# An opening of one core: the scale row's lower half by column quarters, and the first two half units of the MLP interleaved

## The chip, the cores and the metric

The kernel runs on one core of one Trainium2 chip. A core has a matrix engine (TensorE, PE in the rows; PEld is its weight load), VectorE (DVE), ScalarE (ACT), GpSimd (POOL), and SyncE (SP), whose in-order queue issues the loads from memory. Engines run beside each other and meet at semaphores. The metric is the device time of one execution in microseconds (us), here the median of three.

## The reference

Two layers, 256 tokens, 2048 channels, all in fp32. Each layer has a mixer and an MLP, and each of these begins with a norm that a conditioning vector modulates:

```python
cond = jax.nn.silu(c)
for i in range(DEPTH):
    mod = jnp.einsum('bd,sdk->bsk', cond, ada_w[i]) + ada_b[i]       # 2048 x 12288 weights for each layer
    shift_t, scale_t, gate_t = jnp.split(mod[:, 0], 3, axis=-1)
    shift_m, scale_m, gate_m = jnp.split(mod[:, 1], 3, axis=-1)
    h = modulate(rmsnorm(x, norm_g[i, 0]), shift_t, scale_t)          # h * (1 + scale) + shift
    y = pool_mixer(h, ...) if i == 0 else retention(h, ...)
    x = x + gate_t[:, None, :] * y
    h = modulate(rmsnorm(x, norm_g[i, 1]), shift_m, scale_m)
    x = x + gate_m[:, None, :] * sq_relu_mlp(h, mlp_w1[i], mlp_w2[i])
return rmsnorm(x, final_g)
```

The change touches the modulation of the first layer's MLP: `shift_m` and `scale_m` for channels 0 to 1023, and the first columns of `h @ mlp_w1[0]`.

## The kernel before, in words

**Products.** A product of fp32 by fp32 is made of three matmuls on rounded halves (`h_lo` by `w_hi`, `h_hi` by `w_lo`, `h_hi` by `w_hi`, L701). Weights come in chunks of 512 KB: two K tiles of 128 rows by 512 columns, in a ring of four buffers `raw`. ScalarE rounds a chunk into `w_hi` (`hi`, L1167), VectorE subtracts it into `w_lo` (`lo`, L1598), and TensorE runs 12 matmuls on it (2 K tiles, 2 token tiles, 3 products). SP loads the chunk four places on once `lo` of a chunk is done (`load_chunk`, L515).

**The conditioning rows.** A row of 1024 outputs of `cond @ ada_w` is summed from 16 pieces of 512 KB (128 K rows by 1024 columns). They pass through 12 slots: 4 in `ada_raw`, 8 in memory that `h_hi` and `h_lo` (`ada_early_h`) or `a_hi` and `a_lo` (`ada_early_a`) use later. SP loads a piece once the piece 12 places before it is consumed (`load_early`, L521). Some K tiles are multiplied on TensorE (`shared_rows`, L883: two matmuls of 32x512 for a piece, `cond` as the stationary operand), the others are added up on VectorE (`early`, L1628, one instruction of 128x1024), and TensorE sums VectorE's part over the partitions once (`row_blocks`, L853). `LOW_SCALE_PE` (L151) lists the K tiles of the scale row that go to TensorE. Segment 3 is 32 such pieces: 0 to 15 the shift row, 16 to 31 the scale row, both for channels 0 to 1023. In this text scale piece 0 is piece 16 of the segment. When a row is full, ScalarE copies it out (`copy_rows`, L1274), TensorE transposes it (`column`, L953), and VectorE adds the bias (`take_half`, L1737) and makes the gain (`gains`, L1933).

**The norm.** `norm_fill(f)` (L974) transposes and scales two K tiles of x on TensorE (four matmuls of 128x128), with two banks `tb` in turn; ScalarE copies each out (`transposed_x`, L1212) and later modulates it in place (`norm_bank`, L1227), and VectorE splits it into `h_hi` and `h_lo` (`split_h`, L1971). The first K tiles have a shorter way (`split_first`, L1943).

**The order.** After the pooling mixer, TensorE runs the shift pieces, fills 0 to 6 with the scale pieces among them, the column, fill 7, and then 8 parts of the first MLP group. A part is a half unit: 512 columns over the lower 8 K tiles, so 4 chunks (`half_unit`, L750). During the parts 32 more pieces (segment 4) come in among the chunks; most are added up on VectorE. Then come the whole units of both layers. The order on every engine is written out by hand.

## Time and profile before

| | |
|---|---|
| Three runs | 2336.54, 2337.79 (median), 2337.93 us |
| Span of the profiled execution | 2336.1 us; the runs are 0.5 to 1.9 us above it |
| TensorE busy over the span | 2251.9 us (96%) |
| VectorE, ScalarE busy | 1681.1 us (72%), 1084.2 us (46%) |
| Moved by DMA | 664.21 MB, mean 284 GB/s |
| Start of the first MLP part | 188.1 us into the span |

The profile holds one execution. Its rows are read for two things: where TensorE, whose rows make up most of the chain that ends last, stands still, and what it does there besides products. In this kernel both lie in the stretch before 188 us; behind it TensorE is busy nearly without a gap. The DMA queues move 400 GB/s and more up to about 262 us, and less behind that.

### The profile page before, as it was taken

What the parts mean: (1) busy time and instruction counts of PE and PEld (TensorE: products, weight loads), DVE (VectorE), ACT (ScalarE), POOL (GpSimd) and SP (SyncE); (2) the same over time, 40 slices, a digit from 0 to 9 for tenths busy, and PEclk for the clock granted to TensorE, in tenths of its full rate; (3) what the DMA queues carried; (4) which work ended last, traced back from release to release, by engine and by line L of the source; (5) the groups of instructions that cost most, each with busy time, mean ns of one, the idle gap of its engine ahead of it and who ended that gap; (6) DMA issues with size and microseconds to landing.
All of it is one profiled execution on the core that took longest, in us unless ns stands there. A gap on an engine that the chain in (4) does not pass through costs nothing.

```text
span 2336.1 us, 28515 instructions
## 1 busy us (share of the span) xinstructions
PE 2251.9 (96%) x10033; PEld 1817.7 (78%) x10033; DVE 1681.1 (72%) x1814; ACT 1084.2 (46%) x1342; POOL 139.9 (6%) x249
## 2 busy tenths in 40 slices
PE   4489999999999999999999999999999999999998
PEld 2147788888888887888888888887888888888887
DVE  4668889788887898777676767677877555555557
ACT  2324554544544545444454444555553453453454
POOL 0000000100100100001000001000100000000000
PEclk9689999999999999999999999999999999999999
DMA  9999989998998977888766887876997776776774
GB/s 400 415 413 393 339 297 328 364 367 277 368 334 292 362 281 231 303 264 275 246 233 215 299 260 244 273 239 202 333 359 248 235 230 195 226 232 191 232 228 152
DMA packets 276674, 664.21 MB, mean 284 GB/s; under 512 B 21768, under 2 KB 22200, under 8 KB 269632
## 3 DMA queue, kind: packets, MB, share of 16 engines
q1 hardware_dynamic: 260320, 611.92, 75.8%
q0 software_dynamic: 15328, 49.87, 6.2%
q8 instruction: 75, 1.23, 0.2%
q10 hardware_dynamic: 896, 0.75, 0.1%
q14 instruction: 55, 0.45, 0.1%
HBM read 638.30 MB, written 24.14 MB: 284 GB/s over the span
## 4 chain that ended last, share of the span: by engine, by line
PE 88%; DMA 2%; DVE 2%; ACT 1%; issue 0%; POOLq 0%; POOL 0%; SPq 0%; DVEq 0%; ACTq 0%
PE acc L701 86%; DMA raw<-in_mlp_w 2%; PE acc L1122 1%; DVE w_lo L1601 1%; PE score_ps L1109 0%; ACT w_hi L1173 0%; DVE ada_acc L1607 0%; PE score_ps L908 0%; PE tb L848 0%; DVE ev L1903 0%; PE tb L983 0%; DVE x L1907 0%; DVE scratch L1773 0%; DVE scratch L1768 0%; PE mod_ps L856 0%
## 5 line engine op out<-in xcount | busy, mean ns | idle before, releaser
L1601 DVE TENSOR_TENSOR w_lo<-raw,w_hi 128x1024 fp32r<-128x1024 f32 x775 | 943.3, 1223 | 558.6 <-ACT w_hi L1173 555.5
L1173 ACT ACTIVATE w_hi<-raw 128x1024 fp32r<-128x1024 f32 x775 | 821.8, 1061 | 1094.8 <-PE acc L701 971.5
L701 PE MATMUL acc<-w_hi,h_lo 128*128 128x512 f32 x1788 | 698.5, 391 | 2.6 <-issue 1.6
L701 PE MATMUL acc<-w_hi,h_hi 128*128 128x512 f32 x1788 | 695.8, 389 | 0.0
L701 PE MATMUL acc<-w_lo,h_hi 128*128 128x512 f32 x1788 | 695.8, 389 | 0.0
L701 PE MATMUL acc<-w_hi,a_lo 128*128 128x512 f32 x1308 | 511.6, 391 | 0.4 <-DVE w_lo L1601 0.4
L701 PE MATMUL acc<-w_lo,a_hi 128*128 128x512 f32 x1308 | 510.3, 390 | 0.0
L701 PE MATMUL acc<-w_hi,a_hi 128*128 128x512 f32 x1308 | 510.0, 390 | 0.0
L701 PEld LDWEIGHTS acc<-w_hi,h_lo 128*128 128x128 f32 x1788 | 335.7, 188 | 75.1 <-issue 4.1
L701 PEld LDWEIGHTS acc<-w_hi,h_hi 128*128 128x128 f32 x1788 | 335.7, 188 | 70.0
L701 PEld LDWEIGHTS acc<-w_lo,h_hi 128*128 128x128 f32 x1788 | 335.8, 188 | 68.5
L1607 DVE SCALAR_TENSOR_TENSOR ada_acc<-ada_raw,cond,ada_acc 128x1024 f32<-128x1024 f32 x239 | 305.1, 1279 | 10.9 <-DMA ada_raw<-in_ada_w 10.5
L701 PEld LDWEIGHTS acc<-w_hi,a_lo 128*128 128x128 f32 x1308 | 246.6, 189 | 57.7 <-issue 6.1
L701 PEld LDWEIGHTS acc<-w_hi,a_hi 128*128 128x128 f32 x1308 | 246.4, 188 | 51.5
L701 PEld LDWEIGHTS acc<-w_lo,a_hi 128*128 128x128 f32 x1308 | 246.6, 189 | 50.9
L2436 POOL DMA_DIRECT2D square_blocks<-ev x112 | 61.3, 553 | 717.4 <-DVE ev L2161 701.8
L1607 DVE SCALAR_TENSOR_TENSOR ada_acc<-ada_early_h,cond,ada_acc 128x1024 f32<-128x1024 f32 x36 | 44.9, 1281 | 24.4 <-DMA ada_early_h<-in_ada_w 24.3
L878 PE MATMUL mod_ps<-ada_early_h,cond 128*32 128x512 f32 x88 | 18.7, 935 | 28.5 <-DMA ada_early_h<-in_ada_w 28.5
L1470 ACT ACTIVATE ev<-ev 128x512 f32<-128x512 f32 x64 | 36.7, 626 | 0.0
L2167 DVE TENSOR_TENSOR a_lo<-ev,a_hi 128x512 fp32r<-128x512 f32 x56 | 35.8, 680 | 0.0
L1204 ACT ACTIVATE sq_junk<-x 128x512 bf16<-128x512 f32 x45 | 27.8, 618 | 15.6 <-DMA x<-in_x 7.5
L2161 DVE STREAM_TRANSPOSE ev<-ev 128x1024 f32<-128x1024 f32 x28 | 34.7, 1238 | 0.0
(216 smaller groups left out, 912.9 us busy)
## 6 DMA issues: line engine op xcount, KB each, us to landing
raw<-in_mlp_w SPq DMA_DIRECT2D x512, 512.0 KB, 5.1
ada_raw<-in_ada_w SPq DMA_DIRECT2D x248, 512.0 KB, 6.6
raw<-in_ret_w_in SPq DMA_DIRECT2D x192, 512.0 KB, 4.6
ada_early_h<-in_ada_w SPq DMA_DIRECT2D x32, 1024.0 KB, 13.4
raw<-in_ret_w_out SPq DMA_DIRECT2D x64, 512.0 KB, 4.4
ada_raw<-in_ada_w SPq DMA_DIRECT2D x16, 1024.0 KB, 12.5
square_blocks<-ev POOLq DMA_DIRECT2D x112, 128.0 KB, 4.8
ev<-square_blocks POOLq DMA_DIRECT2D x28, 512.0 KB, 6.4
```

Of the source, the lines that this page charges most:

```text
L701: mm = nc.tensor.matmul(acc[pair][t][:], l[:, CK * c + j, tok], w[:, slot, j, :], start=first and j == 0 and i == 0, stop=last and j == CK ...
L878: mm = nc.tensor.matmul(bank[32 * b:32 * b + 32, :], cond[:, k:k + 1].to_broadcast([P, 32]), raw_rows[:, b * NB:(b + 1) * NB], start=first ...
L1122: mm = nc.tensor.matmul(acc[pair][t][:], probs_r[:, half, columns:columns + P], v[:, v_t, :], start=first and i == 0, stop=last and i == 2)
L1173: nc.scalar.activation(w_hi[:, o % RING], raw[:, o % RING], ACT.Copy).then_inc(hi_ready, 1)
L1204: nc.scalar.activation(sq_junk[:, t, :], x[:, t, block_ * NB:(block_ + 1) * NB], ACT.Square, scale=D ** -0.5, accum_out=ssq[:, t, block_:b ...
L1470: nc.scalar.activation(squares_of(u, t, turns), squares_of(u, t, turns), ACT.Square).then_inc(sq_done, 1)
L1601: nc.vector.tensor_tensor(w_lo[:, o % RING], raw[:, o % RING], w_hi[:, o % RING].bitcast(F32), ALU.subtract).then_inc(lo_ready, 1)
L1607: nc.vector.scalar_tensor_tensor(out=part, in0=raw_rows, scalar=cond[:, k:k + 1], in1=part, op0=ALU.mult, op1=ALU.add).then_inc(ada_done, 1)
L2161: nc.vector.transpose(blocks_of(w), blocks_of(w)).then_inc(sq_turned, 1)
L2167: nc.vector.tensor_tensor(by_blocks(a_lo, w, t), turned(w, t), by_blocks(a_hi, w, t).bitcast(F32), ALU.subtract).then_inc(tlo, 1)
L2436: pool.dma_start(there[:, :, q, :].rearrange("r j n -> j r n"), blocks_of(w)[32 * q:32 * q + 32].rearrange("p (r n) -> p r n", r=4)).then_ ...
```

## The change

The 16 pieces of the scale row are cut another way. A piece is now two K tiles by 512 columns, so that 8 pieces fill channels 0 to 511 (the first quarter) and 8 more fill channels 512 to 1023 (the second). Ten of the 16 go to TensorE (before, six), six to VectorE (before, ten). TensorE writes the even and the odd K tiles to separate blocks of a bank, 32 partitions each, and VectorE adds the two blocks with the bias in `take_quarter`, once for each quarter. VectorE's own pieces take two instructions of 128x512, the second of which waits for the first. The first quarter opens K tiles 0 to 3 of h; the four chunks that need only these (the first two of part 0 and of part 1) are loaded among the scale pieces and run first, on both accumulators. The second quarter's pieces, fills 4 to 7 and a second column stand between and behind the chunks.

```diff
-LOW_SCALE_PE = (1, 3, 7, 11, 14, 15)
+LOW_SCALE_PE = (1, 3, 5, 6, 7, 9, 11, 13, 14, 15)
+KQ = KT // 2
+SCALE_SUM_AT = (5, 13)
+FIRST_PAIR = ((0, 0), (0, 1), (1, 0), (1, 1), (0, 2), (0, 3), (1, 2), (1, 3))
+PAIR_LOADED_BEHIND = {22: 0, 23: 1, 26: 2, 28: 3}
+LOW_TURN = 3 * SEG + KT + KQ
...
-            return slot, (ada_early_h if g < 4 * SEG else ada_early_a)[:, slot - RING]
+            return slot, (ada_early_h if g < LOW_TURN else ada_early_a)[:, slot - RING]
...
+                if seg == 3 and a >= KT:
+                    q, i = (a - KT) // KQ, (a - KT) % KQ
+                    sp.dma_start(to.rearrange("p (k n) -> p k n", k=2),
+                                 ada_flat[1, 2 * i * P:(2 * i + 2) * P, 1, q * NB:(q + 1) * NB].rearrange(
+                                     "(k p) n -> p k n", p=P)).then_inc(ada_in[slot], 16)
+                    return
...
             for a in range(SEG):
                 load_early(3, a)
-                if a == 30:
-                    load_chunk(0, first_part(0))
+                if a in PAIR_LOADED_BEHIND:
+                    load_chunk(PAIR_LOADED_BEHIND[a], pair_chunk(PAIR_LOADED_BEHIND[a]))
...
+            def second_quarter():
+
+                scale_rows(30, SEG)
+                norm_fill(4)
+                column(score_ps)
+                norm_fill(5)
...
+            def scale_rows(a0, a1):
+                for a in range(a0, a1):
+                    g, j = 3 * SEG + a, a - KT
+                    q, i = j // KQ, j % KQ
+                    bank, b = ((score_ps, 2), (mod_ps, 0))[q]
+                    if j == SCALE_SUM_AT[q]:
+                        n.add(AD=DVE_BEFORE[g] - n.n["AD"])
+                        pe.wait_ge(ada_done, n.n["AD"])
+                        nc.tensor.matmul(bank[32 * b:32 * b + 32, :], ones[:, 0:32],
+                                         ada_acc[:, AW + q * NB:AW + (q + 1) * NB], start=False, stop=False).then_inc(row_mm, 1)
+                        n.add(RM=1)
+                    if ON_PE[g]:
+                        first = PE_BEFORE[g] == PE_BEFORE[g - i]
+                        if first and q:
+                            pe.wait_ge(row_ready, 3)
+                        slot, raw_rows = early_slot(3, a)
+                        pe.wait_ge(ada_in[slot], early_loads(3, a))
+                        for h in range(2):
+                            mm = nc.tensor.matmul(bank[32 * (b + h):32 * (b + h) + 32, :],
+                                                  cond[:, 2 * i + h:2 * i + h + 1].to_broadcast([P, 32]),
+                                                  raw_rows[:, h * NB:(h + 1) * NB], start=first, stop=i == KQ - 1)
...
+            scale_rows(16, 20)
             pe.wait_ge(gate_ready, 4)
             pe.wait_ge(diag_ready, 1)
-            for f in range(KT // 2 - 1):
-                norm_fill(f)
-                if f in (1, 3):
-                    shared_rows(3, 15 + f, 17 + f)
-                elif f == 5:
-                    shared_rows(3, 20, 28)
-            shared_rows(3, 28, SEG)
+            norm_fill(0)
+            scale_rows(20, 22)
+            norm_fill(1)
+            scale_rows(22, 24)
             column(score_ps)
-            norm_fill(KT // 2 - 1)
-
+            norm_fill(2)
+            norm_fill(3)
+            scale_rows(24, 26)
             n.add(HT=CH)
+            pe.wait_ge(evac, 4 * TT)
+            between = {1: lambda: scale_rows(26, 28), 2: lambda: scale_rows(28, 30), 3: second_quarter,
+                       5: lambda: norm_fill(6), 7: lambda: norm_fill(7)}
+            for s, (i, c) in enumerate(FIRST_PAIR):
+                pe.wait_ge(lo_ready, n.of("U") * HALF + (s + 1))
+                if s == 0:
+                    first_chunk()
+                else:
+                    ready_h(c)
+                    chunk(c, h_hi, h_lo, i, c == 0, c == HALF - 1, slot=s % RING)
+                if s in between:
+                    between[s]()
...
+            def scale_piece(a):
+                q, i = (a - KT) // KQ, (a - KT) % KQ
+                part = ada_acc[:, AW + q * NB:AW + (q + 1) * NB]
...
+                even, odd = raw_rows[:, 0:NB], raw_rows[:, NB:2 * NB]
+                if i:
+                    nc.vector.scalar_tensor_tensor(out=part, in0=even, scalar=cond[:, 2 * i:2 * i + 1], in1=part,
+                                                   op0=ALU.mult, op1=ALU.add).then_inc(scale_step, 1)
...
+                dve.wait_ge(scale_step, scale_steps[0])
+                nc.vector.scalar_tensor_tensor(out=part, in0=odd, scalar=cond[:, 2 * i + 1:2 * i + 2], in1=part,
+                                               op0=ALU.mult, op1=ALU.add).then_inc(ada_done, 1)
```

On TensorE, between the shift pieces and the first matmul of the MLP, this stands in the kernel before (`tb<-diag,x` x4 is one fill, `score_ps<-ada_...,cond` x2 one scale piece, `ada_acc,ones` the sum of VectorE's part, `ident,seg_row` the column):

```order
L983 MATMUL tb<-diag,x 128x128 x8
L908 MATMUL score_ps<-ada_early_h,cond 32x512 x2
L983 MATMUL tb<-diag,x 128x128 x8
L908 MATMUL score_ps<-ada_early_h,cond 32x512 x2
L983 MATMUL tb<-diag,x 128x128 x8
L908 MATMUL score_ps<-ada_early_h,cond 32x512 x2
L908 MATMUL score_ps<-ada_raw,cond 32x512 x2
L983 MATMUL tb<-diag,x 128x128 x4
L856 MATMUL score_ps<-ada_acc,ones 32x512 x2
L908 MATMUL score_ps<-ada_early_h,cond 32x512 x4
L959 MATMUL score_ps<-ident,seg_row 128x128 x4
L983 MATMUL tb<-diag,x 128x128 x4
```

and this in the changed kernel:

```order
L959 MATMUL score_ps<-ada_early_h,cond 32x512 x4
L1033 MATMUL tb<-diag,x 128x128 x4
L949 MATMUL score_ps<-ada_acc,ones 32x512
L959 MATMUL score_ps<-ada_early_h,cond 32x512 x2
L1033 MATMUL tb<-diag,x 128x128 x4
L959 MATMUL score_ps<-ada_early_h,cond 32x512 x4
L1009 MATMUL score_ps<-ident,seg_row 128x128 x4
L1033 MATMUL tb<-diag,x 128x128 x8
L959 MATMUL mod_ps<-ada_raw,cond 32x512 x2
```

Eight fills, six pieces, the sum and the column stood ahead of the MLP; now it is four fills, six pieces (five of the first quarter, one of the second), half the sum and a column. The rest stands among the products. Behind the fourth chunk TensorE of the changed kernel has the second quarter's end (the last rows of the fourth chunk, then two pieces, fill 4, the second column, fill 5, and the fifth chunk):

```order
L721 MATMUL acc<-w_lo,h_hi 128x512
L721 MATMUL acc<-w_hi,h_hi 128x512
L959 MATMUL mod_ps<-ada_early_a,cond 32x512 x4
L1033 MATMUL tb<-diag,x 128x128 x4
L1009 MATMUL score_ps<-ident,seg_row 128x128 x4
L1033 MATMUL tb<-diag,x 128x128 x4
L721 MATMUL acc<-w_hi,h_lo 128x512
```

In the kernel before there is nothing between the chunks there. On VectorE of the changed kernel the same place reads as follows (`w_lo` of two chunks, `take_quarter` and the gain, then the split of K tiles 4 and 5, `w_lo` of the sixth chunk, the split of K tiles 6 and 7, and three pieces of segment 4):

```order
L1684 TENSOR_TENSOR w_lo<-raw,w_hi 128x1024 x2
L1858 TENSOR_TENSOR mod_col<-score_ps,bias_col 128x4
L1860 TENSOR_TENSOR mod_col<-score_ps,mod_col 128x4
L2062 SCALAR_TENSOR_TENSOR gain_col<-mod_col,norm_col 128x4
L2102 CAST h_hi<-scratch 128x512
L2104 TENSOR_TENSOR h_lo<-scratch,h_hi 128x512
L1684 TENSOR_TENSOR w_lo<-raw,w_hi 128x1024
L2102 CAST h_hi<-scratch 128x512
L2104 TENSOR_TENSOR h_lo<-scratch,h_hi 128x512
L1693 TENSOR_SCALAR ada_acc<-ada_early_a,cond 128x1024
L1690 SCALAR_TENSOR_TENSOR ada_acc<-ada_early_a,cond,ada_acc 128x1024 x2
L1684 TENSOR_TENSOR w_lo<-raw,w_hi 128x1024
```

Before, the splits stood ahead of the pieces of segment 4, and `w_lo` of a chunk alternated with one piece of segment 4.

## Rows read from the trace of the kernel before

**Rows 1.** The page: shares of the chain that ended last, by engine.
```profile
PE 88%; DMA 2%; DVE 2%; ACT 1%; issue 0%; POOLq 0%; POOL 0%; SPq 0%; DVEq 0%; ACTq 0%
```
**Rows 2.** Timeline of PE: start, length, operation, count, [idle before, releaser].
```profile
167.17 1.92 PE L856 MATMUL score_ps<-ada_acc,ones 128*32 128x512 f32 x4 [4.37 <-DVE ada_acc L1607]
168.88 1.92 PE L908 MATMUL score_ps<-ada_raw,cond 128*32 128x512 f32 x4
170.73 2.86 PE L983 MATMUL tb<-diag,x 128*128 128x128 f32 x16
...
174.50 2.05 PE L983 MATMUL tb<-diag,x 128*128 128x128 f32 x16
176.48 1.05 PE L908 MATMUL score_ps<-ada_early_h,cond 128*32 128x512 f32 x4
...
182.37 1.05 PE L856 MATMUL score_ps<-ada_acc,ones 128*32 128x512 f32 x4
183.25 1.94 PE L908 MATMUL score_ps<-ada_early_h,cond 128*32 128x512 f32 x8
185.94 0.66 PE L959 MATMUL score_ps<-ident,seg_row 128*128 128x128 f32 x4 [0.75 <-ACT seg_row L1286]
186.44 1.06 PE L983 MATMUL tb<-diag,x 128*128 128x128 f32 x8
188.11 0.47 PE L742 MATMUL acc<-w_hi,h_hi 128*128 128x512 f32 x1 [0.62 <-DVE h_hi L1951]
...
190.93 0.39 PE L701 MATMUL acc<-w_hi,h_lo 128*128 128x512 f32 x1
```
**Rows 3.** Stretches: length, busy us (count) by engine, PE clock, DMA share, GB/s.
```profile
162.00:170.70 8.70, 4.33 (x12) 0.55 (x8) 7.83 (x15) 2.98 (x10) 1.15 (x1) 0.71 1.03 408
170.70:188.10 17.40, 16.05 (x98) 9.92 (x97) 13.92 (x16) 6.54 (x11) 0.00 (x0) 0.95 1.02 381
188.10:210.00 21.90, 21.89 (x97) 18.06 (x97) 20.89 (x24) 12.37 (x17) 0.00 (x0) 1.00 1.04 399
```
**Rows 4.** The chain in order of time, from 243.7 us: start, length, what.
```profile
243.72 9.45 DMA raw<-in_mlp_w
253.19 1.07 ACT w_hi L1173
254.28 1.24 DVE w_lo L1601
...
335.48 508.70 PE acc L701 x2244
```
**Rows 5.** Timeline of PE: the wait at the 25th chunk.
```profile
255.56 0.50 PE L701 MATMUL acc<-w_hi,h_lo 128*128 128x512 f32 x1 [0.54 <-DVE w_lo L1601]
```
**Rows 6.** Timeline of ACT: a chunk rounded, the row copied, two K tiles of x modulated.
```profile
182.97 1.05 ACT L1173 ACTIVATE w_hi<-raw 128x1024 fp32r<-128x1024 f32 x1
185.29 0.60 ACT L1286 ACTIVATE seg_row<-score_ps 128x512 f32<-128x512 f32 x1 [1.27 <-issue]
190.71 1.08 ACT L1235 ACTIVATE scratch<-scratch,mod_col,gain_col 128x256 f32<-128x256 f32 x2
```
**Rows 7.** Timeline of DVE: weights, column, gain, first modulation, splits.
```profile
184.06 1.23 DVE L1601 TENSOR_TENSOR w_lo<-raw,w_hi 128x1024 fp32r<-128x1024 f32 x1 [2.67 <-ACT w_hi L1173]
186.82 0.17 DVE L1744 TENSOR_TENSOR mod_col<-score_ps,bias_col 128x16 f32<-128x16 f32 x1
187.67 0.29 DVE L1951 CAST h_hi<-scratch 128x256 fp32r<-128x256 f32 x1
189.00 0.42 DVE L1977 CAST h_hi<-scratch 128x512 fp32r<-128x512 f32 x1
189.46 0.69 DVE L1979 TENSOR_TENSOR h_lo<-scratch,h_hi 128x512 fp32r<-128x512 f32 x1
207.36 2.60 DVE L1607 SCALAR_TENSOR_TENSOR ada_acc<-ada_raw,cond,ada_acc 128x1024 f32<-128x1024 f32 x2
```
**Rows 8.** Timeline of PE: two shorter waits.
```profile
130.99 1.06 PE L878 MATMUL mod_ps<-ada_raw,cond 128*32 128x512 f32 x8 [1.27 <-DMA ada_raw<-in_ada_w]
141.02 1.30 PE L856 MATMUL mod_ps<-ada_acc,ones 128*32 128x512 f32 x8 [2.31 <-DVE ada_acc L1607]
```
**Rows 9.** Stretches around these two waits, columns as in Rows 3.
```profile
124.70:141.70 17.00, 13.43 (x74) 8.18 (x76) 12.30 (x11) 3.09 (x4) 0.00 (x0) 1.00 1.01 417
141.70:145.10 3.40, 3.40 (x15) 1.17 (x8) 0.93 (x2) 0.00 (x0) 0.00 (x0) 0.50 1.02 408
```

More of the change, by code:

```diff
@@ L1635, in early @@
                         continue
+                    if seg == WIDE_SEGS and half:
+                        scale_piece(a)
+                        continue
                     if k:
@@ L2117, in _ @@
             diagonals()
-            early(3, 18, SEG)
-            n.add(U=2, TB=CH, GN=2)
+            early(3, 18, 24)
+            n.add(U=2, TB=2, GN=2)
             lo(0)
@@ L2122, in _ @@
             second_lo(0)
-            take_half(0)
-            gains(slice(0, KT // 2))
+            take_quarter(0)
+            gains(slice(0, KT // 4))
             split_first()
@@ L2127, in _ @@
             second_lo(1)
+            early(3, 24, 26)
+            lo(2)
+            early(3, 26, SEG)
+            lo(3)
+            lo(4)
+            take_quarter(1)
+            gains(slice(KT // 4, KT // 2))
+            n.add(TB=CH - 2)
             split_h(2)
-            lo(2)
+            lo(5)
             split_h(3)
-            lo(3)
             for i in range(PARTS):
```

108 lines of the change are left out of this document (80 added, 28 removed).

## The prediction, made before the changed kernel was run

> **What bounds the kernel now.** I read the chain by engine first [rows 1]: 88% of it is TensorE, 2% DMA. So a change counts by what it does to TensorE's last matmul. Then TensorE's timeline around the change [rows 2]. The reader is to see that from 170.73 to 188.11 us it has only two waits, 0.75 us for the copied row and 0.62 us for the first split of h; the rest of those 17.4 us is fills, scale pieces, the sum and the column, end to end. The stretch view says the same: 16.05 us busy of 17.40, and 4.33 of 8.70 in the stretch before it [rows 3]. The long wait of this opening, 4.37 us, ends at 167.17, where the shift row waits for VectorE [rows 2], and the change leaves everything up to there as it is.
>
> Behind 188.11 the products run without a gap (21.89 of 21.90 us [rows 3]) at 0.2267 us a matmul (508.70 us by 2244 [rows 4]), 2.72 us a chunk. There the DMA queues are full too, 399 GB/s at a busy share of 1.04 [rows 3], and chunks and the pieces of segment 4 come hardly faster than TensorE uses them: at the 25th chunk it waits 0.54 us for `w_lo` [rows 5], and the chain runs through that chunk's load, 9.45 us from issue to landing, its rounding and its subtraction [rows 4]. So the opening has two limits close together. TensorE has work for nearly all of it, and a TensorE that came to the parts earlier would meet the same bytes at the same rate, and wait at the 25th chunk.
>
> The Trainium skill speaks against the first half of this. Its page "Perfetto Trace Analysis", section "Identifying the Most-Contended Engine", says that a busy share of the matmul row is no measure of how near TensorE is to its limit, since matmuls are pipelined, and that the weight loads are. By it, TensorE with its loads at 9.92 of 17.40 us [rows 3] would have room here. What decides for me is not the share but the starts: each group in the timeline begins where the one before it stops issuing (174.50, then 176.48 [rows 2]), with no releaser named.
>
> **The change, part by part.**
>
> *Durations, by starts.* A piece takes 0.94 us (two from 183.25 to 185.19), a fill 1.0 (two from 174.50 to 176.48), a sum of two matmuls 0.88 (182.37 to 183.25), a column 0.50 (185.94 to 186.44), the first chunk 2.82 (188.11 to 190.93) [rows 2]. At half clock (0.50 from 165.7 on; it is 0.95 in the mean of 170.7 to 188.1 [rows 3]) a piece took 1.85 (168.88 to 170.73) [rows 2].
>
> *Work added on TensorE.* Ten pieces instead of six: 4 x 0.94 = 3.8 us. A second column: 0.5. The sums are two matmuls in both. The first work behind 170.73 is now a piece, which half clock stretches by 0.9 us, where the first two fills lost 0.8 (2.79 against 2.0): 0.1. Together 4.4 us, and none of it is beside other work, since TensorE is in order and has no wait left that it could fill but the 1.4 us above.
>
> *Where the first chunk comes.* From 170.73: pieces 1 and 3 to 173.5, fill 0 to 174.5, half the sum and piece 5 to 175.9, fill 1 to 176.95, pieces 6 and 7 to 178.8. ScalarE copies the row (0.60 [rows 6]) to 179.5, the column is done at 180.0; TensorE goes on with fills 2 and 3 and piece 9 to 183.0. Meanwhile ScalarE has rounded chunk 1 behind fill 1's copy (0.97, to 178.5 [rows 6]), and VectorE subtracts it (1.15, to 179.7), makes `w_hi` of the second chunk and half its `w_lo` (to 181.0), three additions and the gain in place of 0.4 us (0.7, to 181.7), the modulation and the first cast (to 182.5 [rows 7]). So the first chunk starts at 183.0, 5.1 us earlier than 188.11.
>
> *And the fifth.* 2.82 for the first, 2.72 for each of three, piece 11 (0.94) behind the second, half a sum and piece 13 (1.4) behind the third: the fourth ends at 196.35. Pieces 14 and 15 to 198.25. Now the second quarter: copy to 198.9, fill 4 to 199.25, column to 199.75, fill 5 to 200.8; on VectorE take and gain to 200.4, on ScalarE the modulation of two K tiles (1.0 [rows 6]) to 201.4, on VectorE cast and subtraction (0.42 and 0.69 [rows 7]) to 202.6. TensorE waits 1.8 us. The fifth chunk starts at 202.6; before, it started at 190.93 + 3 x 2.72 = 199.1. The head start of 5.1 us has become 3.5 us behind.
>
> *The next three.* VectorE does `w_lo` of the sixth chunk only behind that first split, then the second split, to 205.7; TensorE is there at 205.3 and waits 0.4. Behind this stand three pieces of segment 4 (0.7, then 1.3 each, half of 2.60 [rows 7]) ahead of `w_lo` of the seventh chunk, done at 210.0; TensorE, with fill 6 behind the sixth, is there at 209.4 and waits 0.6. With fill 7 behind the eighth chunk the ninth starts at 216.6. Before, it started at 190.93 + 7 x 2.72 = 210.0. That is 6.6 us later, which the other count confirms: 4.4 of work, plus waits of 0.7 + 1.8 + 0.4 + 0.6 = 3.5 in place of 1.4, is 6.5.
>
> *What is given back.* A TensorE that is 6.6 us late doesn't wait at the 25th chunk: 0.5 less. Net 6.1 us.
>
> *Loads.* The scale pieces' runs in memory are 2 KB as a chunk's are, where they were 4 KB. The stretch of pieces alone moved 408 GB/s, the mixed one 399 [rows 3]; if all of that is the chunks' doing, a 2 KB load costs 0.06 us more, 1.0 us for 16, and nothing if it isn't. Against it, 170.7 to 188.1 moved only 381 GB/s [rows 3], since slots came free late; the new order issues the four chunks among the pieces, where their ring is free, and could win back (408 - 381) x 17.4 / 408 = 1.2 us. Both ends together move the landings by -1.2 to +1.0 us, and with TensorE behind its data that costs nothing. I take 0.
>
> *VectorE's split pieces* are a kind the trace doesn't show (128x512, twice). Bounds: 0.64 each, half of 1.28, up to 1.3 each, if a short one costs as much as a long. Three of them lie ahead of each sum; by the upper end the first sum is late by up to 1 us. I take 0.69, as the 128x512 subtraction [rows 7].
>
> *A wait that the change adds:* `take_quarter` in VectorE's order, with the column behind it on TensorE. Queued behind it: `w_lo` of chunks 6 and on, segment 4's pieces, and through these SP's later loads. The chain above counts it. Loads slip by up to 4 us, which TensorE's own 6.6 covers.
>
> **Sum.** 2336.1 (the span) + 6.1 = 2342.2, and the median run is 1.7 above the span: 2343.9.
>
> **The rivals.**
>
> *The clock falls at the new wait.* A wait of 1.27 us left the clock at 1.0, one of 2.31 was followed by 3.4 us at 0.50, that is 1.2 instead of 2.4 GHz [rows 8, 9]. The new 1.8 us lies between. If it falls, 3.4 us pass at half rate: 1.7 more, 2345.6; for a stretch twice as long 3.4, 2347.3. Against it: TensorE was dense before this wait. The Trainium skill, "TensorE: Matmul & The Clock Gate", section "HAM oscillation — how this bites in real kernels", says that a wait between bursts of matmuls is paid twice, the second time by a throttled clock. By that rule this rival is the likelier; the trace has it both ways.
>
> *The new waits don't arise.* If splits, copies and columns fit beside the fills better than by my count, 4.4 - 1.4 + 0.7 - 0.5 is left: 3.2 us, 2341.0. This is the least that the added matmuls leave. It would show as a fifth chunk at about 200.8.
>
> *The head start is kept (faster).* TensorE reaches the first chunk 5.1 us earlier, and if pieces, fills and column slip in beside the products and the loads are 1.2 us earlier and no longer limit, the end comes up to 5.1 earlier: 2332.7. It decides from the point where the fifth chunk starts ahead of 199.1. Against it: 12 matmuls more than before have to run (8 for pieces, 4 transposes) on an engine whose rows follow end to end [rows 2], and even if they cost nothing, the 25th chunk's load gives no more than 1.2 + 0.5 us, 2336.1. The Trainium skill's rule on the busy share, above, would be the reason for this rival; the starts of the rows are the reason that I hold it unlikely.
>
> **How the numbers follow.** My forecast 0.50, the clock 0.17, no new waits 0.20, head start kept 0.08 (half of it capped by the loads, hence no change), something that I don't see 0.05. A change of 0.2%, 4.7 us, is about what a measurement of this kernel tells from none. Slower by more than that: forecast and clock, less the lower edge of the forecast: 0.62. Within: no waits, that edge, the capped case: 0.29. Faster: 0.09. The range goes from 2338.0 (the case without waits, less 3.0 us: the added 4.4 us of work mis-sized, or the loads' 1.2 and 0.5 won) to 2347.8 (the clock down for the longer stretch, and 0.5 for the runs' spread).
>
> **What the new profile would show.** Right: first matmul of the MLP at 182 to 184 us; two more waits of TensorE behind it, the largest of 1 to 2.5 us ahead of the fifth chunk; the ninth chunk at 215 to 218; no wait at the 25th; ten pieces of 0.94 us. Wrong: a fifth chunk before 199, pieces that take less among the products, or a gap of TensorE behind 220 us. A clock of 0.50 behind 200 us means the first rival.

## The result and the profile after

| | before | after |
|---|---|---|
| Median (lowest to highest) of 10 runs each | 2337.75 us (2336.54 to 2338.72) | 2342.68 us (2341.65 to 2345.39) |
| Ratio, with its 95% interval | | 1.0022 (1.0013 to 1.0031) |
| Profiled execution: span, mean clock | 2336.1 us, 0.987 | 2343.1 us, 0.985 |
| First, fifth, ninth chunk of the MLP starts | 188.1, 199.1, 210.0 us | 181.5, 202.5, 216.8 us |

The kernel became slower by 4.9 us; the forecast was 6.1. The profiled execution of the changed kernel is one of its slower ones (2344.9 us with what lies around its span): its span is 7.0 us above that of the kernel before. At 900 us it is 5.9 us behind (the same transposes start at 900.06 there and at 894.12 before), and the rest comes with a second stretch at half clock behind that, where the kernel before stayed at 1.00 (columns as in [rows 3]):

```profile
902.80:906.20 3.40, 3.40 (x9) 2.63 (x8) 3.33 (x10) 1.53 (x5) 0.55 (x1) 0.50 0.97 336
```

The chain by engine has lost its DMA share, 2% in [rows 1]:

```profile
PE 91%; DVE 1%; issue 1%; ACT 0%; POOLq 0%; POOL 0%; DVEq 0%; ACTq 0%
```

The timeline of PE, which answers to [rows 2] and [rows 5]. Columns are start, length, operation, count, [idle before, releaser]; L959 is a scale piece, L1033 a fill, L949 the sum, L1009 the column:

```profile
167.08 1.07 PE L880 MATMUL score_ps<-ada_acc,ones 128*32 128x512 f32 x2 [4.37 <-DVE ada_acc L1690]
167.11 1.07 PE L959 MATMUL score_ps<-ada_early_h,cond 128*32 128x512 f32 x2
...
170.66 1.95 PE L1033 MATMUL tb<-diag,x 128*128 128x128 f32 x8
172.54 0.62 PE L949 MATMUL score_ps<-ada_acc,ones 128*32 128x512 f32 x1
...
175.47 1.91 PE L959 MATMUL score_ps<-ada_early_h,cond 128*32 128x512 f32 x8
178.12 0.66 PE L1009 MATMUL score_ps<-ident,seg_row 128*128 128x128 f32 x4 [0.75 <-ACT seg_row L1349]
...
181.48 0.50 PE L762 MATMUL acc<-w_hi,h_hi 128*128 128x512 f32 x1
...
195.91 1.91 PE L959 MATMUL mod_ps<-ada_early_a,cond 128*32 128x512 f32 x8
197.75 1.16 PE L1033 MATMUL tb<-diag,x 128*128 128x128 f32 x8
198.75 0.60 PE L1009 MATMUL score_ps<-ident,seg_row 128*128 128x128 f32 x4
199.18 1.06 PE L1033 MATMUL tb<-diag,x 128*128 128x128 f32 x8
202.45 0.47 PE L721 MATMUL acc<-w_hi,h_lo 128*128 128x512 f32 x1 [2.21 <-DVE h_lo L2104]
...
216.76 0.48 PE L721 MATMUL acc<-w_hi,h_lo 128*128 128x512 f32 x1
```

The reader is to see three things. The first scale pieces start at 167.11, 0.03 us behind the shift row's sum, in the midst of it. The first chunk comes 6.6 us sooner than before, with no wait ahead of it. Then one wait of 2.21 us stands between fill 5 and the fifth chunk. The stretches, to set against [rows 3] and [rows 9] (length, busy us and count by engine, PE clock, DMA share, GB/s):

```profile
181.50:202.45 20.95, 18.74 (x88) 11.97 (x87) 11.39 (x19) 8.05 (x13) 0.00 (x0) 1.00 1.04 398
203.07:206.48 3.41, 3.41 (x10) 2.64 (x9) 3.32 (x5) 2.36 (x3) 0.00 (x0) 0.50 1.04 377
216.76:256.00 39.24, 39.24 (x175) 31.57 (x174) 37.74 (x33) 18.18 (x22) 0.00 (x0) 1.00 1.03 394
```

Right behind the wait TensorE ran at 0.50 for 3.41 us, which costs 1.7. From the ninth chunk to 256 us it is busy for 39.24 of 39.24 us; the kernel before was busy for 38.70 us of the same stretch. So the wait at the 25th chunk [rows 5] is gone.

### The profile page after: what moved, and what is told of

It reads as the page before. It is cut to its first block, busy times and chain, and to the rows that moved or that the text cites. A ratio compares the mean times of both kernels' runs of the same rounds, so it can differ in the third digit from the quotient of the medians.

```text
span 2343.1 us, 28564 instructions
## 1 busy us (share of the span) xinstructions
PE 2258.1 (96%) x10053; PEld 1820.5 (78%) x10053; DVE 1676.9 (72%) x1821; ACT 1083.8 (46%) x1343; POOL 139.2 (6%) x249
## 4 chain that ended last, share of the span: by engine, by line
PE 91%; DVE 1%; issue 1%; ACT 0%; POOLq 0%; POOL 0%; DVEq 0%; ACTq 0%
PE acc L721 88%; PE acc L1185 1%; PE score_ps L1172 0%; PE tb L1033 0%; DVE ada_acc L1690 0%; PE tb L872 0%; DVE ev L2028 0%; PE mod_ps L959 0%; DVE w_lo L1684 0%; PE score_ps L932 0%; PE mod_ps L880 0%; ACT w_hi L1236 0%; DVE x L2032 0%; PE score_ps L959 0%; PE tb L857 0%
## 5 line engine op out<-in xcount | busy, mean ns | idle before, releaser
L1690 DVE SCALAR_TENSOR_TENSOR ada_acc<-ada_early_h,cond,ada_acc 128x1024 f32<-128x1024 f32 x30 | 37.2, 1280 | 24.0 <-DMA ada_early_h<-in_ada_w 24.0
```

What stands on the lines that cost most here:

```text
L1690: nc.vector.scalar_tensor_tensor(out=part, in0=raw_rows, scalar=cond[:, k:k + 1], in1=part, op0=ALU.mult, op1=ALU.add).then_inc(ada_done, 1)
```

## The experiments

Each was timed in five rounds beside the kernel before; "above" is its median less that of the kernel before in the same job. An interval of a ratio is 0.0009 wide to each side, 2.1 us, so a difference of under 2 us between two variants is not told by their medians, and what is said of it below comes from the traces. The ninth chunk's start is that of the profiled execution; the chunks behind it run without gaps in all of them, but where it is said. In some profiled executions the shift row's sum stands at 165.3 to 165.5 us instead of 166.8 to 167.3, since the clock did not fall at 141 us there [rows 9]; these have a star, and up to 1.7 us of their earlier ninth chunk is this.

| kernel | median, us | above | ratio (95%) | ninth chunk | longest wait behind the first chunk, and the clock behind it |
|---|---|---|---|---|---|
| the changed kernel | 2342.68 | 4.93 | 1.0022 (1.0013 to 1.0031) | 216.8 | 2.21, 0.50 |
| q2_early | 2339.54 | 1.69 | 1.0008 (0.9999 to 1.0017) | 213.2 | none, 1.00 |
| fill6_in_wait* | 2344.25 | 6.40 | 1.0025 (1.0016 to 1.0035) | 214.6 | 1.35, 1.00 |
| fill6_pieces_later* | 2343.41 | 5.81 | 1.0023 (1.0014 to 1.0032) | 213.0 | 1.32, 1.00 |
| seven_on_pe | 2342.00 | 4.15 | 1.0018 (1.0009 to 1.0027) | 214.9 | 2.22, 0.50 |
| seven_filled* | 2342.10 | 4.68 | 1.0022 (1.0013 to 1.0031) | 214.3 | 0.63, 1.00 |
| q2_and_seven* | 2339.91 | 2.06 | 1.0008 (0.9999 to 1.0017) | 211.9 | 0.61, 1.00 |
| pair_before | 2337.26 | -0.16 | 1.0001 (0.9992 to 1.0010) | 209.5 | none, 1.00 |
| no_pair | 2341.54 | 4.12 | 1.0016 (1.0007 to 1.0025) | 214.9 | 1.32, 1.00 |
| no_pair_four* | 2340.57 | 3.15 | 1.0014 (1.0005 to 1.0023) | 212.1 | 1.72, 1.00 |
| q2_four | 2340.81 | 3.21 | 1.0012 (1.0003 to 1.0022) | 212.0 | 1.41, 1.00 |
| q2_eight_four | 2338.94 | 1.34 | 1.0008 (0.9999 to 1.0017) | 213.1 | 2.18, 0.50 |
| q2_balanced | 2338.86 | 0.98 | 1.0006 (0.9997 to 1.0015) | 211.9 | 0.91, 1.00 |

### q2_early: the second quarter one chunk sooner

```diff
             def second_quarter():
-                scale_rows(30, SEG)
+                scale_rows(28, SEG)
                 norm_fill(4)
                 column(score_ps)
-                norm_fill(5)
-            between = {..., 2: lambda: scale_rows(28, 30), 3: second_quarter, ...}
+            between = {..., 2: second_quarter, 3: lambda: norm_fill(5), ...}
# ScalarE: copy_rows and transposed_x(4) ahead of hi(4); VectorE: take_quarter and gains ahead of lo(4)
```

> The changed kernel, with the second quarter finished one chunk sooner: its last two K tile pieces, fill 4 and the column stand behind the third chunk (they stood behind the fourth), fill 5 alone behind the fourth; ScalarE copies that row ahead of rounding the next chunk, and VectorE takes the quarter ahead of the subtraction of the fifth chunk. TensorE's work is the same. My theory (the 4.9 us are TensorE's work plus the one wait of 2.21 us ahead of the fifth chunk, and the clock that falls behind it): the wait is under 0.5 us, the clock stays at 1.00 until 210 us, the ninth chunk starts at about 212.8 instead of 216.8, and the end comes 2.2 us earlier, 3.9 in executions that had the lowered clock: 2339 to 2340.5, that is 1.5 to 2.8 us above the kernel before. Rival one (the pieces' 2 KB runs and the moved loads set the time): the wait goes, but a new one for w_lo of the fifth to ninth chunk takes its place, and the end is as in the changed kernel, 2342 to 2343. Rival two (the order of fills and columns doesn't matter since later buffers absorb it): also 2342 to 2343, with the ninth chunk earlier and a wait behind it.

Measured: 1.69 us above the kernel before, where the changed kernel is 4.93. No run of the one lies among those of the other (at most 2340.73, at least 2341.65). The waits of TensorE from 160 to 860 us (us in total, times, longest):

```profile
PE score_ps L879 <- DVE ada_acc L1689: 4.4, 1, 4.4
PE score_ps L1008 <- ACT seg_row L1348: 0.7, 1, 0.7
```

Nothing else is left, and the stretch around the later chunks stands at full clock:

```profile
198.00:213.50 15.50, 15.50 (x80) 13.02 (x79) 15.33 (x16) 9.94 (x14) 0.00 (x0) 1.00 1.03 386
```

The ninth chunk starts at 213.2, 3.6 us sooner. So about 3.2 of the 4.9 us, by the medians, were the wait ahead of the fifth chunk and what it drew after it. Both rivals are out.

### fill6_in_wait and fill6_pieces_later: filling the wait

```diff
# fill6_in_wait, on the changed kernel
                 norm_fill(5)
+                norm_fill(6)
-                       5: lambda: norm_fill(6), 7: lambda: norm_fill(7)}
+                       7: lambda: norm_fill(7)}
# fill6_pieces_later, on top of it; VectorE, for j in RING..30
-                    early(4, late_summed(j - 1), late_summed(j))
+                    early(4, max(1, late_summed(j - 1) - 2), max(1, late_summed(j) - 2))
```

> The changed kernel, with fill 6 moved from behind the sixth chunk into the wait ahead of the fifth; nothing else. My theory: the fill (1.0 us) lies in the wait of 2.21 us, which becomes 1.2, and a wait of that length left the clock alone in the kernel before (1.27 us at 131 us). The gain is 1.0 us, and 1.7 more in executions in which the clock fell: 2340.0 to 2341.7. If it's the wait itself that draws the clock down whatever its length, 0.50 shows behind it here too and the gain is 1.0 us alone. If waits of TensorE in this place don't set the end (the rival: loads do), the time is that of the changed kernel, 2342.7, and a wait shows up at the 25th chunk.

> fill6_in_wait, and VectorE keeps two pieces of segment 4 behind its old schedule until the last part, so one of them instead of three stands ahead of w_lo of the seventh chunk. My theory (the new wait of 1.35 us at the seventh chunk in fill6_in_wait is VectorE's queue, 3.3 us of pieces between a split and w_lo): w_lo of the seventh chunk is done 2.4 us earlier, that wait goes, the ninth chunk starts 1.3 us earlier and no other wait stands behind it: 1.3 us less than fill6_in_wait's profiled 2342.4, and 2341.0 to 2343.0 in the median, with fewer executions above 2344. If the seventh chunk's load is what w_lo waits for, the wait stays and the time is 2344.2. If slots that come free two pieces later hold the loads back, a wait shows at the 13th to 25th chunk.

Both missed. The first came out 1.6 us slower in the medians, where I had expected 1.0 less. Its runs scatter from 2341.46 to 2345.65, so the sign isn't certain. The profiled run is one of the faster ones (2342.40), so its trace doesn't tell what the slower ones lose; it shows why there was no gain:

```profile
200.80 0.47 PE L721 MATMUL acc<-w_hi,h_lo 128*128 128x512 f32 x1 [1.33 <-DVE h_lo L2105]
...
208.22 0.50 PE L721 MATMUL acc<-w_hi,h_lo 128*128 128x512 f32 x1 [1.35 <-DVE w_lo L1685]
```

The time that the fill had vacated behind the sixth chunk became a wait for `w_lo` of the seventh. The timeline of DVE names the queue in front of it, 3.3 us of segment 4:

```profile
203.64 0.75 DVE L1694 TENSOR_SCALAR ada_acc<-ada_early_a,cond 128x1024 f32<-128x1024 f32 x1
204.42 2.61 DVE L1691 SCALAR_TENSOR_TENSOR ada_acc<-ada_early_a,cond,ada_acc 128x1024 f32<-128x1024 f32 x2
206.95 1.22 DVE L1685 TENSOR_TENSOR w_lo<-raw,w_hi 128x1024 fp32r<-128x1024 f32 x1
```

With two of those pieces held back the wait is gone, and the ninth chunk starts at 213.0 instead of 214.6, as expected. But the shift row of segment 4 comes later by them, and TensorE pays there, mostly at 272.81:

```profile
272.81 1.05 PE L881 MATMUL mod_ps<-ada_acc,ones 128*32 128x512 f32 x4 [0.89 <-DVE ada_acc L1691]
```

Two waits of 0.28 and 0.89 us take back 1.2 of the 1.6 us, and the median, 2343.41, lies above the 2341.0 to 2343.0 that I had expected. Two pieces moved on VectorE cost TensorE nearly as much later as they gave.

### seven_on_pe, seven_filled, q2_and_seven: less work on TensorE

```diff
# seven_on_pe, on the changed kernel; q2_and_seven is the same on q2_early
-LOW_SCALE_PE = (1, 3, 5, 6, 7, 9, 11, 13, 14, 15)
-SCALE_SUM_AT = (5, 13)
+LOW_SCALE_PE = (1, 3, 7, 9, 11, 13, 15)
+SCALE_SUM_AT = (7, 15)
# fills 0 to 3 ahead of scale_rows(20, 24)
# seven_filled, on seven_on_pe, behind norm_fill(5)
+                for r in range(8):
+                    nc.tensor.matmul(mod_ps[:, ...], x[:, 0, ...], diag[:, 0, :], start=True, stop=True)
```

> The changed kernel with seven of the sixteen scale pieces on TensorE instead of ten (1, 3, 7, 9, 11, 13, 15; 5, 6 and 14 go back to VectorE, two instructions each), the sums at pieces 7 and 15, and fills 0 to 3 ahead of the first quarter's last pieces. My theory (TensorE's added work is on the path, 0.94 us a piece): three pieces less are 2.8 us less; VectorE has 4.7 us more, of which it had idle 4.95 and 6.19 us: a wait for its sum of up to 1 us at each of the two sums. The end is 1 to 2.8 us ahead of the changed kernel's: 2340 to 2341.7. The rival that TensorE's rows aren't full there (pieces run beside others, as pieces 1 and 3 did at 167 us beside the shift row): 0 to 0.5 us earlier, or later by the waits for VectorE, 2342 to 2344.

> Both edits together: the second quarter one chunk sooner, and seven pieces on TensorE. My theory adds the two: 2.2 + 1 to 2.8 us less than the changed kernel, with no lowered clock behind 200 us: 2337.5 to 2339.5, the level of the kernel before; it can't go below it by more than about 0.5 us, since the load of the 25th chunk then ends last again, with a wait of TensorE there of up to 1 us. If it does go below by 2 us or more, that limit by the loads is wrong.

> The kernel with seven scale pieces on TensorE (seven_on_pe), and behind fill 5 eight extra matmuls of 128x128 into a bank that nobody reads, 2 us of work in the wait of 2.22 us ahead of the fifth chunk. They add nothing to the path. It tells why seven_on_pe gained 0.7 us in the medians where its trace, set against the changed kernel's, shows TensorE 1.7 us earlier. My theory (the wait lets the clock fall, 1.6 us lost in 3.4 us at half rate, in all of its executions but in only some of the changed kernel's): the clock stays at 1.00 behind 200 us, and the median is 1.6 us less than seven_on_pe's 2342.0: 2340.4, with runs below its lowest, 2341.34. Rival (the clock isn't what hides the gain; data arrive too late for more): 2342, and a wait stands somewhere behind.

Three pieces less on TensorE, 2.8 us by my price, gave 0.7 us in the medians, and 2342.0 lies outside the expected 2340 to 2341.7. The waits of TensorE in seven_on_pe from 160 to 860 us:

```profile
PE acc L721 <- DVE h_lo L2103: 2.2, 1, 2.2
PE score_ps L949 <- DVE ada_acc L1750: 0.9, 1, 0.9
PE score_ps L1009 <- ACT seg_row L1348: 0.8, 1, 0.8
PE acc L762 <- DVE h_hi L2075: 0.6, 1, 0.6
```

New are the 0.9 for VectorE's sum and the 0.6 ahead of the first chunk; the wait ahead of the fifth chunk is as long as it was. The ninth chunk starts 1.8 us earlier than in the changed kernel. My guess that the lowered clock hid the rest fell with seven_filled: its clock stays at 1.00 behind 200 us, and the median is no lower. Its fifth chunk starts at 200.56, seven_on_pe's at 200.64, although its shift row stands 1.4 us earlier, and a wait of 0.46 follows at the seventh:

```profile
207.97 0.50 PE L721 MATMUL acc<-w_hi,h_lo 128*128 128x512 f32 x1 [0.46 <-DVE w_lo L1686]
```

So this variant is held by VectorE and the loads. Of the 1.7 us that a stretch at half clock costs, only 0.50 show between the fifth and the ninth chunk (13.80 us against 14.30 in seven_on_pe), mostly since a TensorE at full rate arrives at that `w_lo` too soon.

q2_and_seven expected the level of the kernel before and got no further than q2_early. Here the waits that took over are 1.22 us for the load of scale piece 9 and 1.06 for VectorE's sum; behind them the clock stood at 0.50 from 178.66 to 182.07:

```profile
173.65 0.62 PE L948 MATMUL score_ps<-ada_acc,ones 128*32 128x512 f32 x1 [1.06 <-DVE ada_acc L1749]
...
178.18 1.49 PE L958 MATMUL mod_ps<-ada_raw,cond 128*32 128x512 f32 x4 [1.22 <-DMA ada_raw<-in_ada_w]
```

### pair_before: the free pieces in the kernel before

```diff
-            shared_rows(3, 4, 16)
+            shared_rows(3, 4, 20)
...
             for f in range(KT // 2 - 1):
                 norm_fill(f)
-                if f in (1, 3):
-                    shared_rows(3, 15 + f, 17 + f)
-                elif f == 5:
+                if f == 5:
```

> The kernel before, with one edit: the scale pieces 1 and 3 run right behind the shift row's last piece, ahead of fill 0, as in the changed kernel. In the changed kernel those two ran beside the shift row's sum and last piece (all between 167.1 and 170.7 us) and cost nothing, since they write other blocks of 32 partitions. My theory: they are free here too, 1.9 us less on TensorE, so the first chunk starts at about 186.3 instead of 188.1; but the load of the 25th chunk then ends last, its wait grows from 0.54 to about 2.4 us, and the time is 2337.3, at most 0.5 less than before (or 1 more, if the clock falls behind that wait). Rival (TensorE's work alone sets the end, and loads follow the earlier start): 2335.9, and the wait at the 25th chunk stays at 0.5. Rival two (the pieces aren't free behind 128x512 work of their own row): first chunk at 188.1, 2337.8.

The pieces are free here too. The timeline of PE (L856 the shift row's sum, L908 pieces of both rows, L983 fills):

```profile
166.86 1.07 PE L856 MATMUL score_ps<-ada_acc,ones 128*32 128x512 f32 x2 [4.37 <-DVE ada_acc L1605]
166.89 1.07 PE L908 MATMUL score_ps<-ada_early_h,cond 128*32 128x512 f32 x2
...
170.45 6.53 PE L983 MATMUL tb<-diag,x 128*128 128x128 f32 x48
...
181.17 1.05 PE L856 MATMUL score_ps<-ada_acc,ones 128*32 128x512 f32 x4 [1.26 <-DVE ada_acc L1605]
...
183.66 1.05 PE L908 MATMUL score_ps<-ada_early_h,cond 128*32 128x512 f32 x4 [0.58 <-DMA ada_early_h<-in_ada_w]
```

What the fills gained, they wait for: 1.26 and 0.58 us, 1.84 in all, for 1.9 us of saved pieces. The first chunk starts at 187.6, and no difference from the kernel before can be told. The median hits the 2337.3 that I had expected, but by luck. I had the price right and its taker wrong: not the 25th chunk's load, but the sum and a scale piece, 6.5 us ahead of the first chunk. At the 25th chunk no wait of TensorE is listed, where I had expected 2.4 us: the rounding of that chunk, which waits for its load in both kernels, starts at 251.91 instead of 253.19. So the load followed the earlier start, as the rival had it. In the kernel before TensorE, VectorE and the loads all arrived at the scale row nearly together, though TensorE's rows showed no wait for the other two.

### no_pair and no_pair_four: without the interleaving

```diff
# no_pair, on the changed kernel
-FIRST_PAIR = ((0, 0), (0, 1), (1, 0), (1, 1), (0, 2), (0, 3), (1, 2), (1, 3))
+FIRST_PAIR = tuple((i, c) for i in range(2) for c in range(4))
-                scale_rows(30, SEG)
+                scale_rows(26, SEG)      # then fill 4, column, fills 5 and 6
+            between = {1: second_quarter, 2: lambda: norm_fill(7)}
# no_pair_four, on top of it, in scale_rows
+                        nth = PE_BEFORE[g] - PE_BEFORE[g - i]
+                        first = nth < 1 + q
+                        if q:
+                            b = 2 * (nth % 2)
```

> The changed kernel with its quarters kept and the interleaving undone: the four chunks of part 0 run first, then those of part 1. Between the second and third chunk stand the rest of the second quarter's pieces, fills 4 to 6 and the column, fill 7 behind the third. TensorE's work is the same. My theory (work and waits of TensorE set the end, whatever chunk they stand between): pieces to about 192, fills to 195.5, the split of K tiles 4 and 5 at about 196.5 (row copied at 192.6, column 193.4, then the 3.3 us from column to h_lo that the changed kernel has), a wait of 0.5 to 1 us, ninth chunk at about 214, no lowered clock: 2340.3 to 2341. Rival (the interleaving is what covers the second quarter): a wait of over 2.5 us ahead of the third chunk, with a clock at 0.50 behind it, and 2343 to 2345.

> The same, and TensorE's pieces of the second quarter write two pairs of blocks in turn (9, 13 and 15 to blocks 0 and 1; 11 and 14 to blocks 2 and 3, the sum to block 2), so that neighbours are in different blocks; VectorE adds four blocks (two instructions of 0.2 us more). My theory from the changed kernel's opening (matmuls of 32 columns into different blocks run beside each other): sum, 13, 14 and 15 take 1.8 us together instead of 3.6; the row is complete 1.8 us sooner, and the end comes 1.4 to 1.8 us ahead of no_pair's. If it's only the change of row, and not the block, that let pieces 1 and 3 go beside the shift row, these take 3.6 us as before and the time is no_pair's, plus 0.4.

no_pair is 0.8 us less above the kernel before than the changed kernel: with the chunks of part 0 and part 1 one after the other, no loss shows. The wait ahead of the third chunk is 1.32 us, its clock stays at 1.00. Its ninth chunk starts at 214.9, 0.9 later than expected, most of it a wait of 0.99 us for VectorE's sum. So alternating parts aren't what the time depends on. That it is how late the second quarter is placed I take from q2_early; no_pair moved both at once, and no run changes the order of the parts alone.

The second quarter's group in no_pair, and then in no_pair_four:

```profile
189.26 0.62 PE L950 MATMUL mod_ps<-ada_acc,ones 128*32 128x512 f32 x1 [0.99 <-DVE ada_acc L1750]
...
192.82 1.16 PE L1034 MATMUL tb<-diag,x 128*128 128x128 f32 x8
```

```profile
187.29 0.62 PE L950 MATMUL mod_ps<-ada_acc,ones 128*32 128x512 f32 x1 [1.00 <-DVE ada_acc L1753]
...
189.67 1.16 PE L1037 MATMUL tb<-diag,x 128*128 128x128 f32 x8
```

Sum and three pieces took 3.56 us where neighbours share their blocks, 2.38 where they don't. That is two thirds of the 1.8 us that I expected, and the medians show 1.0 of it. It is the block that decides, not the row.

### q2_four, q2_eight_four, q2_balanced: towards the kernel before

```diff
# q2_four: q2_early and no_pair_four's blocks.  q2_eight_four, on top of it:
-LOW_SCALE_PE = (1, 3, 5, 6, 7, 9, 11, 13, 14, 15)
+LOW_SCALE_PE = (1, 3, 5, 7, 9, 11, 13, 15)      # sums at 7 and 15, fill 2 ahead of scale_rows(22, 24)
# q2_balanced, on top of that; SyncE: the fifth chunk ahead of segment 4's first four pieces
-            hi(4)                # ScalarE
             norm_bank(2)
+            hi(4)
-            lo(4)                # VectorE
             split_h(2)
+            lo(4)
# and one piece of segment 4 held back on VectorE up to the 15th chunk
```

> The second quarter one chunk sooner (as q2_early), and its pieces on TensorE in two pairs of blocks in turn, as in no_pair_four, where a group of sum and three pieces (189.72 to 192.8 there, 187.7 to 189.7 here) was 1.2 us shorter. My theory (TensorE's work sets the end as long as no data are late): the group of seven matmuls and the sum takes 2.4 instead of 3.6 us, fourth and later chunks start 1.2 us earlier than in q2_early, and the first h of that quarter, at about 198, isn't waited for, since the fourth chunk and fill 5 stand ahead of it: 2338.3 to 2338.7, 1.0 above the kernel before. The rival, from seven_filled and fill6_in_wait (each saved a wait ahead of the fifth chunk and got one of 0.45 and 1.35 us at the seventh, for VectorE's w_lo): a wait ahead of the seventh chunk takes up to 1 us of it, 2339.0 to 2339.5, no difference from q2_early.

> The same with eight pieces on TensorE (1, 3, 5, 7, 9, 11, 13, 15), sums at pieces 7 and 15, fill 2 ahead of the first quarter's last pieces. TensorE has 0.94 us less in the first quarter, and less than that in the second. If TensorE's work alone set the end, this would be 0.9 to 1.8 us under q2_four. By the other theory (in this opening VectorE's pieces, the loads of 1.3 us each and TensorE's work all end within 1 to 2 us of each other, as pair_before showed, where 1.7 us less of TensorE became waits of 1.26 for VectorE's sum and 0.58 for a load) it becomes waits of that kind at 173 and 188 us, and the time is q2_four's within 0.5. This is also the candidate for a version level with the kernel before, 2337.5 to 2338.5.

> q2_eight_four, which waits 2.18 us ahead of the fifth chunk (and then has 3.41 us at half clock), with three moves and no matmul more or less: SyncE loads the fifth chunk ahead of segment 4's first four pieces (it landed at 195.27, behind them); ScalarE modulates K tiles 4 and 5, and VectorE splits them, ahead of the fifth chunk's rounding and subtraction, which had waited for that load with the split queued behind them; VectorE keeps one piece of segment 4 back until the 15th chunk of the MLP. My theory (the wait is that load, through the in-order queues of ScalarE and VectorE): the load lands at about 190, h_lo at 196.7, the wait is under 0.5 us and no clock falls; the ninth chunk starts at 209.6 to 210.5, where the kernel before had 210.0, and the time is 2336.5 to 2337.8, level with the kernel before. It can't be more than about 1 us below that kernel: the loads up to the 25th chunk are the same bytes at the same rate, and a wait comes up there. If the fifth chunk isn't set by the load but by the column's chain (take_quarter, gain, modulation, split, 3.3 us), the wait stays over 1 us, and the time is 2338 to 2339. If it is 2335.5 or less, the limit by the loads was wrong.

q2_four missed. The group was shorter as expected, and the ninth chunk starts at 212.0, 1.2 sooner than in q2_early, but 1.0 of this stands at the first chunk already (180.92 against 181.90), where the half clock had come later. What the group gained was taken: a wait of 1.41 us stands ahead of the fifth chunk. The median is 1.3 above q2_early's. The wait's cause is in the timeline of ACT:

```profile
195.48 1.06 ACT L1238 ACTIVATE w_hi<-raw 128x1024 fp32r<-128x1024 f32 x1 [1.31 <-DMA raw<-in_mlp_w]
196.45 2.06 ACT L1300 ACTIVATE scratch<-scratch,mod_col,gain_col 128x256 f32<-128x256 f32 x4
```

ScalarE stood before the fifth chunk, whose load had not landed, with the modulation of h queued behind it. Where the median's loss lies I can't say: the profiled execution was at 0.50 for 3.41 us at 898 and again at 1632 us, where every kernel has the same waits of 0.35, 0.34 and 0.80 us; most others pass there at 1.00. I have no run that tells why.

q2_eight_four waits 2.18 us for the same load, has the lowered clock behind it, and still is only 1.34 above. Its median is 1.9 under q2_four's, though its ninth chunk starts 1.1 later: traces and medians disagree here, and the waits for VectorE's sum at 173 and 188 us that I had expected are absent. q2_balanced takes that wait away by order alone: 0.91 us are left, for `w_lo` of the fifth chunk, and the clock stays up.

```profile
196.18 0.43 DVE L2111 CAST h_hi<-scratch 128x512 fp32r<-128x512 f32 x1 [1.23 <-ACT scratch L1303]
196.64 0.69 DVE L2113 TENSOR_TENSOR h_lo<-scratch,h_hi 128x512 fp32r<-128x512 f32 x1
197.25 1.22 DVE L1689 TENSOR_TENSOR w_lo<-raw,w_hi 128x1024 fp32r<-128x1024 f32 x1
```

The ninth chunk starts at 211.9, not at 209.6 to 210.5, and the median, 2338.86, is 0.98 above and outside the expected 2336.5 to 2337.8: the split now comes first on VectorE, and the subtraction behind it is late. The limit by the loads was not reached (no wait at the 25th chunk), so that claim of mine stays untested. No version beats the kernel before. The intervals of pair_before, q2_balanced, q2_early, q2_eight_four and q2_and_seven all contain 1, so none of the five can be told from it.

## Why the prediction was right, and where its steps were not

**The end.** Forecast +6.1 us, measured +4.93, within the range and slower as said. The sum came out nearly right for reasons that are partly others, so part of it is luck. The profiled execution stands 5.9 us behind at 900 us with 1.7 of clock in it, which the main forecast doesn't hold; without the clock it would be 4.2 by this trace. How many of the other executions had the lowered clock behind the fifth chunk is not on record.

**The first chunk** was forecast at 183.0 and came at 181.5. The step that failed is the 3.8 us for "ten pieces instead of six", with "none of it is beside other work". Pieces 1 and 3 write blocks 2 and 3 of a bank while the sum and last piece of the shift row write blocks 0 and 1; all are done by 170.66, when before the shift row alone was done by 170.73 [rows 2]. The added work was overcounted there by two pieces, 1.9 us. pair_before shows the same, and no_pair_four that neighbours in other blocks are what it takes. The Trainium skill states the like: "TensorEngine Tiling (Array Packing)", section "Key Properties", says that different tiles of the array can load weights and multiply in parallel. I had not weighed that page; the trace agrees (starts at 167.08 and 167.11).

**The sum** cost more than I counted: I split 0.88 us in two halves of 0.44. But before, its two matmuls went to two blocks beside each other. A sum for one block takes as long as one for two: with its piece it stands from 172.54 to 174.38, 1.84 us, as much as two pieces. That is 0.9 us more for the two sums.

**The fifth chunk** was forecast at 202.6 behind a wait of 1.8 us, and came at 202.45 behind 2.21. q2_early, without that wait, confirms the mechanism: this step carried the forecast, though its length was 0.4 short. TensorE was early at it and still had to wait, since the wait ends with the second quarter's chain (last piece, copy, column, gain, modulation, split) and that had been placed behind the fourth chunk.

**The small waits of 0.4 and 0.6 us** at the sixth and seventh chunk didn't show: TensorE was at half clock there. In seven_filled and fill6_in_wait, with the clock at 1.00, the one at the seventh appears, 0.46 and 1.35 us, behind the three pieces of segment 4 that the prediction named.

**The clock** was the first rival, and it happened in the profiled execution: 3.41 us at 0.50 behind 2.21 us of waiting, a price of 1.7 where I wrote 1.7. It stands beside the main mechanism, not in place of it. The Trainium skill, "TensorE: Matmul & The Clock Gate", section "HAM oscillation — how this bites in real kernels", counts the wait and the penalty of the lowered clock behind it as separate parts of a kernel's time; here seven_filled shows that the second is partly covered by VectorE's lateness. Its example is of waits of 3 to 5 us, longer than the 1.8 forecast, so "by that rule this rival is the likelier" was more than the section gives. By the profiled execution alone the ninth chunk at 216.8 matches my 216.6, by errors that cancel: 1.9 too much for pieces against 0.9 too little for sums, 0.4 too little for the wait, and 1.7 of clock that the forecast had left to a rival, less the 1.0 of small waits that didn't come.

**The loads.** The prediction took 0 between -1.2 and +1.0. No wait of TensorE behind 160 us names a load in the changed kernel, so 0 was right for it. But "no wait left that it could fill", said of TensorE alone, hid that loads and VectorE were as late as TensorE: every variant that took work off TensorE (seven_on_pe, q2_and_seven, pair_before, q2_four) got part of it back as waits for them. The changed kernel's ACT timeline had the sign of it, the rounding of the fifth chunk behind its load:

```profile
195.37 1.06 ACT L1236 ACTIVATE w_hi<-raw 128x1024 fp32r<-128x1024 f32 x1 [9.47 <-DMA raw<-in_mlp_w]
```

And the queues weren't at "400 GB/s and more" all the way to 262 us, as the text on the profile before has it: the rows give 381 from 170.7 to 188.1 us and 399 behind [rows 3].

**VectorE's split pieces** were taken at 0.69 us each and took 0.75, at 0.79 from start to start. The first three pieces are six instructions, done at 172.2 us, and delayed no sum. (The 0.97 and 1.15 us that the prediction takes for a chunk's rounding and subtraction aren't in the rows it names, which show 1.05 and 1.23; neither decided the sum.) The last two, and what stands behind them:

```profile
170.66 0.75 DVE L1745 SCALAR_TENSOR_TENSOR ada_acc<-ada_early_h,cond,ada_acc 128x512 f32<-128x512 f32 x1
171.45 0.75 DVE L1751 SCALAR_TENSOR_TENSOR ada_acc<-ada_early_h,cond,ada_acc 128x512 f32<-128x512 f32 x1
177.15 1.23 DVE L1684 TENSOR_TENSOR w_lo<-raw,w_hi 128x1024 fp32r<-128x1024 f32 x1 [4.95 <-ACT w_hi L1236]
```

**The 25th chunk** gave back its wait: forecast 0.5, and from the ninth chunk to behind it the distance between the two kernels shrank by 0.8. Its reason, that TensorE comes late, isn't shown to be needed: the wait is gone in pair_before too, where TensorE is at the ninth chunk 0.5 us earlier than before.

## What to carry to other kernels

An engine without waits isn't the only limit when others arrive at the same point: before counting saved or added work at its full price, look how long each other engine and load had been done when it was needed. A head start is worth nothing if the next thing that opens work is still placed for the old time; move the chain that ends the later wait, not the work in front of it. And before adding durations of narrow matmuls, look which blocks of partitions they write.

## What the hardware showed beyond what I expected

- Matmuls with 32 output columns run beside each other when they write different blocks of 32 partitions, across instructions, and one after the other in the same block. Sum and three pieces took 3.56 us in the same two blocks and 2.38 in four.
- The same wait has it both ways: the one of 2.3 us at 141 us [rows 8], which thirteen of the fourteen profiled executions have, was followed by 0.50 in nine of them. At 131 us seven executions waited 1.94 to 1.98 us, and one of them (q2_and_seven) was at 0.50 behind it. In the opening, behind single waits of 2.21, 2.22 and 2.18 us (the changed kernel, seven_on_pe, q2_eight_four) it stood at 0.50 for 3.41 us; behind 1.32, 1.33, 1.41 and 1.72 us (no_pair, fill6_in_wait, q2_four, no_pair_four) it stayed at 1.00. In q2_and_seven 1.06, 0.75 and 1.22 us within 6 us were followed by 0.50. The waits of 0.35, 0.34 and 0.80 us near 900 us were followed by 0.50 in three profiled executions of fourteen, and the same three waits near 1630 us in two.
- A switch between matmuls of 32 and of 128 columns costs a little: chunks between pieces took 2.8 to 3.0 us in the changed kernel instead of 2.72.
